# Shift and scale by column quarters, input projection by K quarters, in a one-core block of three feed-forward stages

## The chip, the core and the metric

The kernel runs on one core of a Trainium2 chip. The core has a matrix engine (PE), a vector engine (DVE), a scalar engine (ACT), a general engine (POOL) and a sync engine (SP), each with its own instruction stream, and 16 DMA engines that they share. Engines wait for one another through semaphores. The metric is the device time of one execution in microseconds (us), taken as a median of several runs.

## What is computed

The reference is a model block on a sequence of 256 rows of 2048 floats. Only its first part matters here:

```
mod = silu(c) @ w_ada + b_ada                      # w_ada: 2048 x 12288
shift1, scale1, gate1, shift2, scale2, gate2 = split(mod, 6)
h = rms_norm(x, norm1_w) * (1 + scale1) + shift1   # 256 x 2048
p = h @ w_in                                       # w_in: 2048 x 4112
u_f, q, k, v, o, gates = split(p)
y_f = real(fft2(u_f));  y_m = mlstm_bidirectional(q, k, v, gates) * sigmoid(o)
x = x + gate1 * (concat(y_f, y_m) @ w_out)
h2 = rms_norm(x, norm2_w) * (1 + scale2) + shift2
... three feed-forward blocks and a second mixer, all from h2 on
```

## The kernel before

Everything is float32. A product at nearly full precision is made of three matmuls on float32r operands: both operands are split into a high part (ACT, `w_hi`) and the rest (DVE, `w_lo`, "split"), and high by high, high by low and low by high are summed. Weights are read once from memory, in units of 1 MB (128 partitions by 2048 floats), into a ring of four slots, `stage`. SP issues these loads in one fixed order; each waits until the unit four before it in the ring is free. A unit that is split is free once DVE has made its low part (`split_made`); a unit that PE reads directly (of w_ada, since it meets only the one vector silu(c)) is free once PE has used it (`ada_used`). `w_hi` and `w_lo` hold two units each, so the split of unit n starts when PE has finished unit n-2.

The stages before the first feed-forward block are:

1. The front. SP loads the shift1 and scale1 columns of w_ada, 32 units of 128 rows by 2048 columns (`ada`, PE line 2643), 16 for each. The row of sums (four bands of 512, one bank of PSUM) is copied by DVE (`copy_sum`), turned into columns by PE (`turn_sum`, line 2655) and added to the bias (`take_sum`). Meanwhile x is normalized, its transposes are made (line 2492), and a table of small vectors comes in over POOL's queue and is transposed (line 2673).
2. The input projection. With shift and scale complete, DVE and ACT make the operand `xt` in eight groups (`norm_finish`). Then 16 units of w_in by column tiles (`in_tiles`, 128 columns by all of K, 48 matmuls of 256 columns each, lines 2394 to 2396), and 16 by rows (`in_rows`, 24 matmuls of 512 columns, lines 2443 to 2447). A result is accumulated in PSUM over all of K and copied once. Beside this, POOL issues the gate1 and scale-and-shift2 columns as 60 pieces of 512 KB into a ring of four (`late_ring`), and DVE multiplies and adds each into an accumulator (`late`, lines 1677 and 1678); four double pieces at the end go to PE. DVE's stream also carries the gates of the mLSTM.
3. The Fourier transform and the four mLSTM heads, with 16 units of scale2 columns that PE uses between them (`ada2`, `scale_units`).
4. The output projection `out1`, 16 units by rows; at its unit 9 DVE starts on the residual sum (`add_gated`), and the reload of x (POOL, line 531) has come by then.

The order on each engine is written by hand in the functions of `build`; nothing is reordered by a compiler.

## Time and profile before

| | us |
|---|---|
| median of 3 runs | 3562.35 |
| lowest and highest | 3561.05, 3566.18 |
| the profiled execution | 3561.49 |
| its span in the trace | 3559.6 |
| first matmul of the input projection | 108.5 |
| Fourier stage begins | 319.3 |
| out1 begins, ends | 387.1, 481.7 |

The span is counted from the first record of the trace; 1.9 us of the execution lie around it. PE is busy for 96% of the span, so a change can only shorten what lies in stretches in which PE is idle or does cheap work, above all the front. The trace lists for each instruction its start, its length and what ended the idle time before it. The granted clock of PE is either full (1.00) or half (0.50) in each moment; a window's value is the mean.

### The profile page before, as it was taken

The page shows a single profiled execution, that of the slowest core. Times are in us where ns is not written, and L with a number is a line of the kernel's source. Part 1 is how long each engine was busy: PE and PEld are TensorE (multiplying, and loading weights), DVE is VectorE, ACT ScalarE, POOL GpSimd, SP SyncE. Part 2 cuts the span into 40 slices and gives each one's busy share as a digit, 9 for nine tenths or more (in the row PEclk, how much of TensorE's full clock was granted, in tenths as well). Part 3 has the DMA queues.
Part 4 walks back from the last instruction along what each step waited for, and adds up shares of the span by engine and source line. Part 5 has one row for each costly group of instructions (what it writes and reads, how often), then busy time and mean ns, then how long its engine had stood idle before and what let it go on. Part 6 is the DMA issues. An engine that isn't in the chain of part 4 may idle for free.

```text
span 3559.6 us, 45278 instructions
## 1 busy us (share of the span) xinstructions
PE 3403.8 (96%) x18458; PEld 2863.0 (80%) x18458; DVE 2017.6 (57%) x2010; ACT 1528.3 (43%) x1554; POOL 346.1 (10%) x411
## 2 busy tenths in 40 slices
PE   5899889999999999999999899999999999999998
PEld 1786678888888888888888799898888788888886
DVE  0674657775566554444444579895455644444445
ACT  1333346653455443333333455663443443333333
POOL 1110000000000000000000137671000000000000
PEclk7899999999999999999999999999899999999999
DMA  9998657777666556976555655667226555665564
GB/s 398 296 340 311 219 172 224 223 223 226 189 187 192 189 196 177 207 199 197 193 189 189 166 150 157 168 174 249 86 96 191 175 189 189 189 190 190 190 190 139
DMA packets 543073, 713.09 MB, mean 200 GB/s; under 512 B 13127, under 2 KB 382079, under 8 KB 535360
## 3 DMA queue, kind: packets, MB, share of 16 engines
q1 hardware_dynamic: 517504, 627.09, 56.7%
q0 software_dynamic: 20624, 79.44, 7.9%
q10 hardware_dynamic: 4784, 4.27, 0.4%
q8 instruction: 120, 1.97, 0.2%
q14 instruction: 41, 0.34, 0.0%
HBM read 698.94 MB, written 11.80 MB: 200 GB/s over the span
## 4 chain that ended last, share of the span: by engine, by line
PE 79%; DVE 9%; ACT 4%; DMA 4%; issue 3%; POOL 1%; ACTq 0%; SPq 0%; DVEq 0%; POOLq 0%
PE ps L2585 9%; PE ps L2587 9%; PE ps L2586 9%; PE ps L2443 9%; PE ps L2444 8%; PE ps L2447 8%; PE ps L2375 7%; PE ps L2376 3%; DVE w_lo L1372 3%; ACT w_hi L812 3%; DMA stage<-in_w_ada 3%; PE ps L2394 2%; PE ps L2396 2%; PE ps L2395 2%; PE ps L2407 1%
## 5 line engine op out<-in xcount | busy, mean ns | idle before, releaser
L1372 DVE TENSOR_TENSOR w_lo<-stage,w_hi 128x2048 fp32r<-128x2048 f32 x528 | 1221.4, 2313 | 1176.0 <-ACT w_hi L812 1175.2
L812 ACT ACTIVATE w_hi<-stage 128x2048 fp32r<-128x2048 f32 x528 | 1010.7, 1914 | 1567.3 <-PE ps L2587 575.9
L2585 PE MATMUL ps<-w_hi,xt 128*128 128x512 f32 x1408 | 552.3, 392 | 3.4 <-DVE xt L1423 1.8
L2586 PE MATMUL ps<-w_lo,xt 128*128 128x512 f32 x1408 | 549.6, 390 | 0.0
L2587 PE MATMUL ps<-w_hi,xt 128*128 128x512 f32 x1408 | 549.6, 390 | 0.0
L2375 PE MATMUL ps<-xt,w_hi 128*128 128x512 f32 x1320 | 472.3, 400 | 6.2 <-DVE w_lo L1372 6.2
L2443 PE MATMUL ps<-w_hi,hid_hi 128*128 128x512 f32 x1152 | 449.6, 390 | 5.9 <-DVE w_lo L1372 5.9
L2444 PE MATMUL ps<-w_lo,hid_hi 128*128 128x512 f32 x1152 | 448.3, 389 | 0.0
L2376 PE MATMUL ps<-xt,w_lo 128*128 128x256 f32 x1320 | 371.3, 281 | 0.0
L2394 PE MATMUL ps<-xt,w_hi 128*128 128x256 f32 x1184 | 342.9, 290 | 18.6 <-DVE w_lo L1372 16.0
L2447 PE MATMUL ps<-w_hi,hid_lo 128*128 128x512 f32 x1152 | 354.6, 389 | 0.0
L2395 PE MATMUL ps<-xt,w_hi 128*128 128x256 f32 x1184 | 337.6, 285 | 0.0
L2396 PE MATMUL ps<-xt,w_lo 128*128 128x256 f32 x1184 | 337.4, 285 | 0.0
L2585 PEld LDWEIGHTS ps<-w_hi,xt 128*128 128x128 f32 x1408 | 265.4, 188 | 59.1 <-issue 2.3
L2587 PEld LDWEIGHTS ps<-w_hi,xt 128*128 128x128 f32 x1408 | 265.4, 188 | 55.6
L2586 PEld LDWEIGHTS ps<-w_lo,xt 128*128 128x128 f32 x1408 | 265.5, 189 | 54.7
L2375 PEld LDWEIGHTS ps<-xt,w_hi 128*128 128x128 f32 x1320 | 248.7, 188 | 66.9 <-DVE w_lo L1372 9.7
L2443 PEld LDWEIGHTS ps<-w_hi,hid_hi 128*128 128x128 f32 x1152 | 216.2, 188 | 52.6 <-DVE w_lo L1372 4.3
L2394 PEld LDWEIGHTS ps<-xt,w_hi 128*128 128x128 f32 x1184 | 229.5, 194 | 29.9 <-issue 23.6
L2376 PEld LDWEIGHTS ps<-xt,w_lo 128*128 128x128 f32 x1320 | 250.1, 189 | 3.6
L2447 PEld LDWEIGHTS ps<-w_hi,hid_lo 128*128 128x128 f32 x1152 | 216.2, 188 | 45.1
L2444 PEld LDWEIGHTS ps<-w_lo,hid_hi 128*128 128x128 f32 x1152 | 216.3, 188 | 44.4
(422 smaller groups left out, 4060.4 us busy)
## 6 DMA issues: line engine op xcount, KB each, us to landing
stage<-in_w_in SPq DMA_DIRECT2D x92, 1024.0 KB, 5.7
stage<-in_w_up SPq DMA_DIRECT2D x88, 1024.0 KB, 5.7
stage<-in_ffn_w_gate SPq DMA_DIRECT2D x88, 1024.0 KB, 5.1
stage<-in_ffn_w_up SPq DMA_DIRECT2D x88, 1024.0 KB, 5.1
stage<-in_ffn_w_down SPq DMA_DIRECT2D x88, 1024.0 KB, 5.4
stage<-in_w_ada SPq DMA_DIRECT2D x48, 1024.0 KB, 8.7
stage<-in_w_down SPq DMA_DIRECT2D x44, 1024.0 KB, 5.5
late<-in_w_ada POOLq DMA_DIRECT2D x64, 512.0 KB, 6.7
```

The lines of the kernel that those rows point to most:

```text
L812: act.activation(w_hi[:, u % 2 * UNIT:(u % 2 + 1) * UNIT], slot(u % SLOTS), ACT.Copy).then_inc(hi_made, 1)
L1372: dve.tensor_tensor(w_lo[:, part], slot(u % SLOTS), w_hi[:, part].bitcast(F32), ALU.subtract).then_inc(split_made, 1)
L2375: pe.matmul(dst, wh, both(k), start=k == 0, stop=False)
L2376: last = pe.matmul(dst[:, T:2 * T], wl, chunk(xt_hi, k), start=False, stop=False)
L2394: pe.matmul(dst, wh, chunk(xh, k0 + k), start=start and k == 0, stop=False)
L2395: pe.matmul(dst, wh, chunk(xl, k0 + k), start=False, stop=False)
L2443: pe.matmul(rows_cols(half, m, n, 512, swapped), a, wh, start=st, stop=False)
L2444: pe.matmul(rows_cols(half, m, n, 512, swapped), a, wl, start=False, stop=False)
L2447: last = pe.matmul(rows_cols(half, m, n, 512, swapped), b, wh, start=False, stop=en)
L2585: pe.matmul(dst, chunk(xt_hi, k, m), wh, start=k == 0, stop=False)
L2586: pe.matmul(dst, chunk(xt_hi, k, m), wl, start=False, stop=False)
L2587: last = pe.matmul(dst, chunk(xt_lo, k, m), wh, start=False, stop=k == KC - 1)
```

## The change

It changes only the stages up to and with out1.

- **Order of loads.** The 32 units of w_ada for shift1 and scale1 are cut otherwise: 512 columns by 512 rows, so that eight units (four of each) hold one quarter of shift and scale. w_in is cut the same way: unit n is K quarter n // 8, column block n % 8. The loads of quarter q+1 of w_ada and of K quarter q of w_in take turns (`IN_PLACE`, `ADA_PLACE`). All 32 units of w_in have 2 KB rows, where half had 512 B and half 4 KB.
- **The projection.** `in_unit` makes one K quarter of a block of 512 columns in a pair of banks. The first eight blocks are copied by ACT to where the result lies (`first_part`), the 24 others are added into it by DVE (`add_part`).
- **Quarters of shift and scale.** `turn_quarter` on PE sums the four bands with a matmul by `four_rows`, `quarter_scale`, `quarter_hi` and `quarter_lo` make four of the sixteen chunks of `xt`.
- **The rest of w_ada.** The shift2 columns, formerly pieces over POOL, are now units on SP's queue like scale2: `ada2` has 32 units instead of 16, eight in turns with the last K quarter, 24 between Fourier stage and heads. The gate1 pieces (32) remain, in a ring of two instead of four; DVE handles 8 in the last K quarter, 8 in the Fourier stage, 4 in the heads, 12 in out1. `fold_rows`, the turn and the bias of gate1 move from the projection into out1, between units 6 and 8, and PE waits for `mod_made` 7 before the second half. x is reloaded after that, and `add_gated` stands at unit 13 instead of 9.

On PE, the place is the end of the first loads of w_ada. Before, from the end of the 12th unit to the first matmuls of the projection (line 2643 is w_ada, 2492 the transposes of x, 2655 the turn of the sums):

```order
L2643 MATMUL ps<-stage,csilu 32x512 x8
L2492 MATMUL ps<-ident,f_nat 128x128 x16
L2643 MATMUL ps<-stage,csilu 32x512 x8
L2492 MATMUL ps<-ident,f_nat 128x128 x12
L2643 MATMUL ps<-stage,csilu 32x512 x64
L2655 MATMUL ps<-ident,mod_row_98 128x4 x4
L2655 MATMUL ps<-ident,mod_row_99 128x4 x4
L2492 MATMUL ps<-ident,f_nat 128x128 x4
```

After, from the fifth unit of w_ada on (2800 is w_ada, 2843 the table, 2615 the transposes of x, 2787 the turn, 2828 the projection):

```order
L2800 MATMUL ps<-stage,csilu 32x512 x20
L2843 MATMUL ps<-ident,rowtab 128x128
...
L2800 MATMUL ps<-stage,csilu 32x512 x12
L2615 MATMUL ps<-ident,f_nat 128x128 x8
L2787 MATMUL ps<-four_rows,mod_row_98 128x1 x4
L2787 MATMUL ps<-four_rows,mod_row_99 128x1 x4
L2828 MATMUL ps<-xt,w_hi 128x256
```

The projection stood behind 128 matmuls of w_ada and now stands behind 32; the table's transposes stand behind five units instead of twelve.

On DVE, the place is out1, from the last part of the operand on. Before (1372 is the split of a unit, 1451 and 1454 the residual sum):

```order
L1383 TENSOR_TENSOR xt_52<-turn_65,xt_52 128x2x256
L1372 TENSOR_TENSOR w_lo_51<-stage_49,w_hi_50 128x2048 x6
L1451 TENSOR_TENSOR f_nat_56<-ps,row_57 128x1024 x2
L1454 TENSOR_TENSOR x_nat_53<-x_nat_53,f_nat_56 128x1024 x2
L1372 TENSOR_TENSOR w_lo_51<-stage_49,w_hi_50 128x2048 x7
```

After (1447 is the split, 1753 a gate1 piece, 1781 and 1787 the copy of its sum and its bias):

```order
L1753 SCALAR_TENSOR_TENSOR acc_g1_106<-late1_101,csilu_62,acc_g1_106 128x1024
L1447 TENSOR_TENSOR w_lo_51<-stage_49,w_hi_50 128x2048
L1753 SCALAR_TENSOR_TENSOR acc_g1_106<-late0_100,csilu_62,acc_g1_106 128x1024
L1753 SCALAR_TENSOR_TENSOR acc_g1_106<-late1_101,csilu_62,acc_g1_106 128x1024
L1753 SCALAR_TENSOR_TENSOR acc_g1_106<-late0_100,csilu_62,acc_g1_106 128x1024
L1753 SCALAR_TENSOR_TENSOR acc_g1_106<-late1_101,csilu_62,acc_g1_106 128x1024
L1447 TENSOR_TENSOR w_lo_51<-stage_49,w_hi_50 128x2048 x2
L1781 COPY mod_row0_98<-ps 128x512
L1447 TENSOR_TENSOR w_lo_51<-stage_49,w_hi_50 128x2048
L1787 TENSOR_TENSOR mod_60<-ps,cols_59 128x16
L1447 TENSOR_TENSOR w_lo_51<-stage_49,w_hi_50 128x2048 x4
```

These rows are the splits of units 6, 7 and 8, 9 and the following; ahead of them a pair of pieces stands before each of the splits of units 4, 5 and 6. The splits stood alone before.

The diff, its core:

```
+IN_PLACE = (0, 2, 4, 6, 9, 12, 14, 15)
+ADA_PLACE = (1, 3, 5, 7, 8, 10, 11, 13)
+def in_place(n):
+    q, i = divmod(n, 8)
+    return 8 + 16 * q + (IN_PLACE[i] if q < 3 else 2 * i)
+def ada_place(a):
+    q, i = divmod(a, 8)
+    return i if q == 0 else 8 + 16 * (q - 1) + ADA_PLACE[i]
+def ada2_place(v):
+    return 57 + 2 * v if v < 8 else 64 + v
...
@@ SP
+        def fetch(at, src, whole, count, used):
+            if freed[at % SLOTS]:
+                sp.wait_ge(*freed[at % SLOTS])
+            ...
+            freed[at % SLOTS] = (used, count)
...
+        for v in range(8, 2 * KC):
+            fetch_ada2(v)
         load("out1", 8, 2, rows(I["w_out"], 0, 8))
@@ POOL
-        for n in (1, 2, 0, *range(3, 64)):
-            if n >= 4:
-                pool.wait_ge(S["late_acc"], n - 3)
...
+        pool.wait_ge(S["norm_xhat"], 2)
+        pool.wait_ge(split_used, 24)
+        for n in range(2):
+            late_piece(n)
...
+        for n in range(2, 32):
+            pool.wait_ge(S["late_acc"], n - 1)
+            late_piece(n)
+        pool.wait_ge(S["mod_made"], 7)
...
@@ ACT
+        def first_part(n):
+            act.wait_ge(split_used, n + 3)
+            for h in range(2):
+                last = act.activation(part_of(n, h), part_bank(n, h), ACT.Copy)
+            last.then_inc(S["tile_copied"], 1)
...
+            if 2 <= n < 10:
+                first_part(n - 2)
+            split_in(n)
+            if i == 0:
+                quarter_hi(q)
+            elif i == 7 and q < 3:
+                copy_sums(q + 1)
@@ DVE
+        for n in range(32):
+            q, i = divmod(n, 8)
+            if n >= 10:
+                add_part(n - 2)
+            if i == 0:
+                quarter_scale(q)
+            split_in(n)
+            if i == 0:
+                quarter_lo(q)
+            if q == 3:
+                late(i, 1)
...
+            late(8 + 2 * g, 2)
...
             last.then_inc(S["pt_made"], 1)
+            late(16 + h, 1)
...
         split("out1", 16, 0, 1)
+        late(20, 2)
...
+        late(22, 2)
         for u in range(4, 16):
             split("out1", 16, 0, u)
-            if u == 9:
+            if u < 6:
+                late(16 + 2 * u, 2)
+            elif u == 6:
+                late(28, 4)
+            elif u == 8:
+                copy_sum(7, 0, ADA + 2 * KC + 1)
+            elif u == 9:
+                take_sum(2, bank(7, 0, 16), 7)
+            if u == 13:
                 dve.wait_ge(S["x_in"], 32)
@@ PE
+        for q in range(3):
+            for step in range(16):
+                if step in IN_PLACE:
+                    i = IN_PLACE.index(step)
+                    in_unit(8 * q + i)
+                    if i == 2:
+                        norm(0, range(2 * q + 2, 2 * q + 4))
+                    elif i == 6:
+                        turn_quarter(q + 1)
+                else:
+                    ada(8 * (q + 1) + ADA_PLACE.index(step))
...
-            scale_units((0, 3, 6, 8)[g], (3, 3, 2, 2)[g])
+            for v in ((8, 9, 10), (11, 12, 13), (14, 15), (16, 17, 18))[g]:
+                ada2(v)
...
-                scale_units(10 + 2 * h, 2)
+                for v in ((19, 20, 21, 22, 23), (24, 25, 26, 27), (28, 29, 30, 31))[h]:
+                    ada2(v)
...
-        rows_half("out1", 8, 0, 0, at_out1, units=range(2, 8), ready=S["mix_lo"])
+        rows_half("out1", 8, 0, 0, at_out1, units=range(2, 7), ready=S["mix_lo"])
+        pe.wait_ge(S["late_acc"], 32)
+        fold_rows(7, late_acc[0][:, :])
+        rows_half("out1", 8, 0, 0, at_out1, units=range(7, 8), ready=S["mix_lo"])
+        turn_sum(7, 0, 0, 7)
+        pe.wait_ge(S["mod_made"], 7)
```

## Rows read from the trace of the kernel before

**Rows 1.** The profile's first page: the span.

```profile
span 3559.6 us, 45278 instructions
```

**Rows 2.** Windows by stage: bounds, length, busy us and count of each engine, PEclk, DMA share, GB/s.

```profile
0.00:44.00 44.00, 19.40 (x89) 2.58 (x89) 1.62 (x3) 8.96 (x9) 14.07 (x32) 0.75 0.98 374
44.00:108.50 64.50, 41.73 (x222) 12.10 (x223) 7.74 (x18) 3.17 (x3) 1.05 (x2) 0.69 1.05 393
108.50:319.30 210.80, 201.21 (x1274) 175.61 (x1274) 153.99 (x125) 76.83 (x64) 33.23 (x61) 0.98 0.94 314
319.30:387.10 67.80, 56.02 (x316) 32.86 (x312) 32.69 (x102) 23.01 (x51) 1.76 (x3) 0.92 0.83 310
387.10:481.70 94.60, 91.37 (x400) 74.52 (x400) 53.30 (x41) 34.53 (x29) 0.54 (x1) 0.98 0.58 179
```

**Rows 3.** Timeline of PE in the front: start, length, line, operation, idle before.

```profile
30.17 1.88 PE L2643 MATMUL ps<-stage,csilu 128*32 128x512 f32 x8 [0.54 <-DMA stage<-in_w_ada]
...
47.27 1.51 PE L2673 MATMUL ps<-ident,rowtab 128*128 128x128 f32 x6
...
99.53 3.57 PE L2655 MATMUL ps<-ident,mod_row 128*128 128x4 f32 x16 [0.81 <-DVE mod_row L1706]
...
108.52 0.55 PE L2394 MATMUL ps<-xt,w_hi 128*128 128x256 f32 x1 [3.88 <-DVE w_lo L1372]
```

**Rows 4.** Timeline of POOL and DVE in the front.

```profile
26.46 0.41 POOL L488 COPY rowtab<-hval 32x64 f32<-32x64 f32 x2 [16.58 <-DMA hval<-in_ssm_log_dt]
...
103.22 0.26 DVE L1712 TENSOR_TENSOR mod<-ps,cols 128x16 f32<-128x16 f32 x2 [3.74 <-PE ps L2655]
...
106.13 2.29 DVE L1372 TENSOR_TENSOR w_lo<-stage,w_hi 128x2048 fp32r<-128x2048 f32 x1
108.34 0.99 DVE L1528 TENSOR_SCALAR turn<-ps,scale_cols,mod 128x256 f32<-128x256 f32 x2
```

**Rows 5.** Timeline: two neighbouring high halves by tiles, two low halves in out1.

```profile
147.58 1.92 ACT L812 ACTIVATE w_hi<-stage 128x2048 fp32r<-128x2048 f32 x1 [3.58 <-PE ps L2396]
...
153.34 1.91 ACT L812 ACTIVATE w_hi<-stage 128x2048 fp32r<-128x2048 f32 x1 [3.58 <-PE ps L2396]
...
428.48 2.29 DVE L1372 TENSOR_TENSOR w_lo<-stage,w_hi 128x2048 fp32r<-128x2048 f32 x1 [3.15 <-ACT w_hi L812]
433.92 2.29 DVE L1372 TENSOR_TENSOR w_lo<-stage,w_hi 128x2048 fp32r<-128x2048 f32 x1 [3.15 <-ACT w_hi L812]
```

**Rows 6.** Groups by line, 108.4 to 319.3 us and Fourier to out1: busy, mean ns.

```profile
L1678 DVE SCALAR_TENSOR_TENSOR acc_g<-late,csilu,acc_g 128x1024 f32<-128x1024 f32 x30 | 37.6, 1280 | 2.8 <-DMA late<-in_w_ada 2.6
...
L2655 PE MATMUL ps<-ident,mod_row 128*128 128x4 f32 x16 | 2.0, 249 | 0.3 <-ACT mod_row L1061 0.3
```

**Rows 7.** DMA issues at 1700:1800, 125:215, 500:620, 300:345; last, FFN pieces: KB, us to landing.

```profile
stage<-in_ffn_w_gate SPq DMA_DIRECT2D x9, 1024.0 KB, 5.1
...
late<-in_w_ada POOLq DMA_DIRECT2D x33, 512.0 KB, 6.7
...
late_f<-in_w_ada POOLq DMA_DIRECT2D x12, 512.0 KB, 5.0
...
stage<-in_w_ada SPq DMA_DIRECT2D x12, 1024.0 KB, 7.9
...
DMA to landing us min/median/max: 3.9/4.9/9.1
```

**Rows 8.** Timeline of PE: Fourier stage begins, last scale2 unit, out1 begins.

```profile
319.34 3.72 PE L2746 MATMUL ps<-dft,projt 128*128 128x256 f32 x16
...
370.53 1.04 PE L2643 MATMUL ps<-stage,csilu 128*32 128x512 f32 x8
...
387.13 0.76 PE L2443 MATMUL ps<-w_hi,xt 128*128 128x512 f32 x1 [3.23 <-issue]
```

**Rows 9.** Windows: loads of w_ada with the queue full; a wait and the clock.

```profile
340.00:345.00 5.00, 4.07 (x35) 2.20 (x34) 1.53 (x3) 2.00 (x6) 0.00 (x0) 1.00 1.01 424
...
350.00:355.00 5.00, 3.91 (x6) 1.67 (x6) 3.80 (x11) 1.06 (x1) 0.00 (x0) 0.50 0.15 62
```

**Rows 10.** Timeline of DVE: the last low half of the operand in out1.

```profile
411.03 0.69 DVE L1383 TENSOR_TENSOR xt<-turn,xt 128x512 fp32r<-128x512 f32 x1 [0.70 <-ACT xt L1075]
```

More of the change, by code:

```diff
@@ L70, in stream_plan @@
 def stream_plan():
-    order = [("in_tiles", 16, 16), ("in_rows", 16, 16), ("ada2", KC, 0), ("out1", 16, 16)]
+    order = [("in", 32, 32), ("ada2", 2 * KC, 0), ("out1", 16, 16)]
     def ffn(n):
@@ new lines, in quarter_hi @@
+        def quarter_hi(q):
+            act.wait_ge(S["mod_made"], q + 1)
+            for g in (2 * q, 2 * q + 1):
+                act.wait_ge(S["norm_turned"], g + 1)
+                if g >= 2:
+                    act.wait_ge(S["norm_done"], g - 1)
+                c = 2 * g + 1
+                link.then(act.activation(turn[:, g % 2 * 512 + T:(g % 2 + 1) * 512], bank(5, g % 2 * T, T),
+                                         ACT.Identity, scale=scale_cols[:, c:c + 1], bias=mod[:, c:c + 1]))
+                act.wait_ge(S["norm_scaled"], g + 1)
+                act.activation(duo(xt_hi, g), turned_duo(g), ACT.Copy).then_inc(S["norm_hi"], 1)
@@ L1734, in _, with split_in @@
-        for b in range(2):
-            take_sum(b, bank(7, 16 * b, 16), 2)
-        scale_of(0)
-        norm_finish(0, scale_cols[:, 0:KC], mod[:, 0:16], lambda g: split("in_tiles", 4, 0, 0) if g == 2 else None)
-        piece = 0
-        for t in range(1, 16):
-            split("in_tiles", 4, t // 4, t % 4)
-            count = 0 if t < 2 else 3 if 6 <= t < 10 else 2
-            late(piece, count)
-            piece += count
-        dve.memset(v_one[:, :].rearrange("p (k n) -> p k n", n=257)[:, :, 256:257], 1.0)
+        def split_in(n):
+            dve.wait_ge(hi_made, n + 1)
+            part = slice(n % 2 * UNIT, (n % 2 + 1) * UNIT)
+            dve.tensor_tensor(w_lo[:, part], slot(in_place(n) % SLOTS), w_hi[:, part].bitcast(F32),
+                              ALU.subtract).then_inc(split_made, 1)
@@ L1798, in _ @@
-        dve.wait_ge(S["ec_made"], 1)
-        dve.tensor_copy(ecols[:, :], bank(2, 0, 32)).then_inc(S["ec_copied"], 1)
-        copy_sum(3, 0, ADA + 2)
+        for n in (30, 31):
+            add_part(n)
+        dve.wait_ge(S["f_act"], 2)
+        link.then(dve.scalar_tensor_tensor(out=two(lfrow[:, :]), in0=fgates, scalar=0.0,
+                                           in1=two(crow[:, :]), op0=ALU.min, op1=ALU.subtract))
+        for d in range(2):
+            last = dve.tensor_tensor_scan(way(rows1, 2 + d, d), ones1[:, :], way(lfrow, d, d), 0.0,
+                                          ALU.mult, ALU.add)
@@ L1801, in _ @@
+        link.then(last)
+        link.then(dve.tensor_tensor(two(rows1[:, 0:512]), igates, two(rows1[:, 512:1024]), ALU.subtract))
+        for d in range(2):
+            last = dve.tensor_tensor_scan(way(rows1, 4 + d, d), ones1[:, :], way(rows1, d, d), NEG,
+                                          ALU.mult, ALU.max)
+        link.then(last)
+        dve.tensor_tensor(rows1[:, 512:1024], rows1[:, 512:1024], rows1[:, 1024:1536],
+                          ALU.add).then_inc(S["f_dve"], 1)
         for g in range(4):
```

420 lines of the change are left out of this document (219 added, 201 removed).

## The prediction

> **What bounds the kernel now.** I read the windows by stage first [rows 2]. The front lasts 108.5 us; its DMA share is 0.98 and 1.05 while PE is busy in only 19.40 of 44.00 and 41.73 of 64.50 us, so loads bound it: nothing of the projection can start before 32 MB of w_ada are in. From 108.5 us to 319.3 PE is busy 201.21 of 210.80 us: the projection is bound by PE. The next stage, up to out1, is mixed (PE 56.02 of 67.80, DMA share 0.83). In out1 PE is busy 91.37 of 94.60 us, at a DMA share of 0.58. All later stages read what they read before, so the sum goes up to the end of out1, at 481.7 of a span of 3559.6 [rows 1].
>
> Then I read the timeline of the front, to see the chain that lets the projection start [rows 3, 4], the rhythm of the units [rows 5], the price of one piece or turn [rows 6], the time from issue to landing [rows 7], and two places in the tail [rows 8, 10].
>
> **Term 1, the start.** The eighth unit of w_ada is used at 30.17, with PE at half clock (1.88 us a unit) [rows 3]. The changed PE stream has the table's transposes after its fifth unit, and these wait for POOL's copy at 26.46 [rows 4]: 26.9, plus 1.5 for the transposes, plus three units of 1.9, is 34.1. Copies of two sums on ACT, bounded by 0.7 each (a DVE pass over as many columns, [rows 10]): 35.5. The transposes of x run beside them. The turn has eight matmuls, 3.57 at this clock [rows 3]: 39.1. Bias, scale and two affine steps, 0.26 + 0.2 + 0.2 + 0.99: 40.8. The split, 2.29, and the first low part, 0.7: 43.8 [rows 4, 10]. The first projection matmul comes at 43.8 instead of 108.52, so 64.7 us earlier. Were the first 2 KB-row loads as slow as one per 3 us, it would be 47.
>
> **Term 2, the projection.** Sixteen blocks with 256-column matmuls at 5.76 us (153.34 minus 147.58) and sixteen with 512 at 5.44 [rows 5] are 92.2 + 87.0 = 179.2, as before. The other 31.6 of the 210.8 us are 9.6 idle, six weighing units of 1.06, one turn of 1.0 (2.0 for two, [rows 6]), and 14.6 that stay: the gates' matmuls and stretches at half clock. New are 32 units of w_ada between the blocks, 33.9 at 1.06; three turns of eight matmuls, 6.0; 24 transposes of x, 3.0 (half of the 0.25 each that 1.51 for six gives at low clock). Copying and adding into place is on ACT and DVE: per unit DVE has 2.29 for the split and two additions of about 0.7, 3.7 of some 6.5 us, and the additions run while ACT makes the next high half, so I take nothing for them; with that cover gone they would cost 1.4 per unit.
>
> The ring adds a wait. The load of block 4 of a quarter takes the slot of a w_ada unit that PE uses just before block 3. From there a load of 5.1 [rows 7], the high half of 1.92 and the low half of 2.29 [rows 4, 5] make 9.4 us with the hops, while PE has only block 3 and two units, 7.9. That is 1.5 idle. Block 5 has the same pattern with 7.6 us of cover and a load that lands behind another one: about 1.9; block 6, after those waits, 0.6. Four us per quarter, three quarters, 12. Bounds: 6 with landings of 4.5, 27 with 6.7, which is what a smaller piece took beside other loads [rows 7]. I take 5.1, since these loads have the same shape, 2 KB rows, and 1 MB.
>
> Term 2 is 179.2 + 14.6 + 33.9 + 6.0 + 3.0 + 12 = 248.7, minus 0.6 for transposes that leave it: the projection ends at 291.9 instead of 319.3. Of the 64.7 us, 27.4 are left.
>
> **Term 3, Fourier stage and heads.** PE has 24 weighing units here instead of 16, and DVE 12 gate1 pieces on a queue of its own. With the queue full, DMA moves 424 GB/s at a share of 1.01 [rows 9], so 1 MB takes 2.49 us. Unit 8 is used about 4.2 us after the stage begins (two Fourier groups ahead of it); only then is unit 12 issued, and from there 20 MB for PE and 6 MB of pieces have to pass: 26 times 2.49 is 64.7. Add 3 us for the last landing and 1.1 for its use: 73.0. Before, out1 began 15.6 us after the end of the last such unit (387.13 minus 371.57, [rows 8]), and that chain is unchanged: 88.6 instead of 67.8, a loss of 20.8. Bounds: with room for everything only the eight more units count, 8.5; with DVE standing at `late` in front of `take_sum` and of the first exponents, which PE awaits through `mod_made` 5, another 5 on top.
>
> **Term 4, out1.** DVE reaches the end of the operand at 411.72 [rows 10]; with pieces 20 and 21 ahead of it I put 413.7 on the old scale. Then pieces 22 to 31. The ring holds two, so piece n is issued when n-2 is weighed, and one step costs a landing plus 1.28 [rows 6]. Landings were 6.7 in the projection and 5.0 in the feed-forward stage [rows 7]; out1 is nearer to the latter in load, so 5.2, a step of 6.5. Piece 22 is done at 415.0, 30 at 441.0, 31 at 442.3. The split of unit 7 stands behind them: 444.6; PE has then waited since unit 6. Unit 7 ends at 450.0. The second half waits for `mod_made` 7, which DVE sets only after the split of unit 9, and this waits for unit 7: 1.92 + 2.29 + 0.4 more, 454.6. Before, unit 8 began at 481.7 minus eight times 5.44, 438.2. A loss of 16.4, which I round to 17 with the wait that unit 3's split adds. Behind the waiting DVE are queued the splits that PE needs next; behind the waiting PE, all of the second half. The reload of x and the row of gate1 start then, with 3 MB or 7.5 us of transfer at 2.49 a MB [rows 9] and their latencies, and some 22 us before unit 12 is over: hidden; if not, `add_gated` delays the split of unit 14.
>
> **A rule of the Trainium skill against term 4.** These pieces took 5.0 and 6.7 us from issue to landing [rows 7]. The Trainium skill, "DMA: Bandwidth & Descriptors", section "Anatomy of one DMA — SWDGE (gpsimd) path", fits 2.0 us plus the bytes at 436 GB/s, which for 512 KB is an estimate of 3.2. With it the step would be 4.5, less than a unit, and DVE would keep up with PE; term 4 would be about 6.8. The trace does not agree for these queues, even its shortest landing is 3.9.
>
> **The sum.** 0 - 27.4 + 20.8 + 17 = +10.4. On the profiled execution's 3561.49 this gives 3571.9; the median of the runs lies 0.86 above the profiled one, so 3572.8, rounded to 3573. Later stages start from the same state and keep their lengths.
>
> **Rivals.**
> First, the pieces keep up. The shortest landing of a gate piece was 3.9 [rows 7]; with it a step is 5.2, under the 5.44 of a unit, DVE never holds PE, and term 4 is the fold and turn, 2.1, and the wait for `mod_made` 7, 4.6: 7. The sum is 0.4: 3563. Speaking for it is the DMA share of 0.58 in out1 [rows 2]; against it, that a median landing in a comparable load is 5.0. Chance 0.20.
>
> Second, landings are as long as where both queues are busy, 6.7 for a piece and 7.9 for a unit [rows 7]. Four steps cost 6 more, the ring of the projection 5 more: 3584. For it is that the projection has the pieces of the last quarter and loads at an even demand of 16 MB per some 60 us. PE waits of 3 to 5 us may also bring the clock down to half, as after the wait at 350 [rows 9], 2.5 us each. Chance 0.22.
>
> Third, and faster than before: the tail is bound by its chains, not by bytes. Then the 24 units and the pieces find room beside the four Fourier groups and the heads, term 3 is 8.5 and term 4 is 7: -27.4 + 15.5 = -11.9, 3551. It decides at 26 MB in some 52 us, 2.0 us each; the row at a share of 1.01 says 2.49, so the chance is 0.08.
>
> My forecast, 3566 to 3581, has 0.50. That the change does not start the projection early is excluded by PE's order.
>
> **How the numbers follow.** A measurement of this kernel can tell 0.2%, 7.1 us, from no change. Slower by more: 0.40 of the forecast (above 3569.5) and all of the second rival, 0.62. Within: 0.10 of the forecast, 0.17 of the first rival, 0.27. Faster: 0.03 of the first and 0.08 of the third, 0.11. The range takes in the first rival and most of the second, 3554 to 3591; the third, and a second rival at its bounds for all terms, are left out.
>
> **What would show it.** In the changed profile: first projection matmul at 44 (wrong above 50); projection over by 292, with PE idle 1 to 2 us for `w_lo` at blocks 4 and 5 of each of three quarters; out1 beginning at 380; DMA share near 1 in the stage before; PE waiting in out1 between units 6 and 7 for more than 5 us and between 7 and 8 for 3 to 4; out1 ending at 492. The prediction is wrong if the weighing units between the blocks cost more than 1.06, if additions on DVE end after the next high half, or if the pieces land in under 4.2 us.

## The result and the profile after

The changed kernel takes 3600.34 us (median of 4 runs, 3599.45 to 3602.30); the kernel before took 3562.96 beside it. The ratio is 1.0105, with a 95% interval of 1.0087 to 1.0122: slower by 37.4 us, where the prediction was slower by 10.4, in a range that ended at 3591. The sign was right, the size was not, and the time lies above every case that was worked out.

The windows of the changed kernel, cut at the same events as [rows 2]: first projection matmul, first Fourier matmul, first scores of the heads, first matmul of out1, last of out1. The columns are bounds, length, busy us and count of each engine, PEclk, DMA share, GB/s.

```profile
0.00:45.30 45.30, 21.07 (x95) 6.70 (x95) 7.29 (x19) 15.36 (x17) 13.43 (x30) 0.97 0.99 347
45.30:302.10 256.80, 239.21 (x1539) 188.81 (x1539) 120.24 (x118) 80.59 (x73) 6.39 (x12) 0.97 0.79 280
302.10:346.80 44.70, 31.05 (x201) 19.19 (x201) 21.29 (x30) 13.02 (x28) 3.71 (x7) 0.81 0.93 372
346.80:404.90 58.10, 44.52 (x184) 21.89 (x185) 30.57 (x92) 12.79 (x22) 2.64 (x5) 0.76 0.80 301
404.90:518.40 113.50, 99.72 (x416) 79.10 (x416) 68.40 (x55) 34.62 (x29) 7.74 (x13) 0.91 0.72 215
```

The same cut of the kernel before, whose last-but-one stage is split here at its first scores:

```profile
319.30:345.60 26.30, 25.37 (x189) 16.01 (x185) 5.37 (x11) 7.61 (x25) 1.06 (x2) 1.00 0.91 362
345.60:387.10 41.50, 30.65 (x129) 16.85 (x128) 27.32 (x91) 15.40 (x26) 0.70 (x1) 0.87 0.78 277
```

Stage by stage the change gives 63.2 us in front, and costs 45.9 in the projection (256.7 instead of 210.8), 18.4 in the Fourier groups, 16.7 in the heads and 18.9 in out1; 1.4 lie behind out1. The sum is +38.1, the difference of the spans (3597.7 and 3559.6). Against the forecast the misses are: start +1.5, projection +8.6, groups and heads together +14.3 (102.9 for 88.6), out1 +1.9 (113.5 for 111.6), the rest +1.4.

The start is as forecast, at 45.34 for 43.8 (timeline of PE; answers to [rows 3]):

```profile
45.34 0.55 PE L2828 MATMUL ps<-xt,w_hi 128*128 128x256 f32 x1 [4.51 <-DVE xt L1458]
```

Where PE waited behind the projection (waits of PE, 302 to 520 us: who waited, for whom, us in total, times, longest):

```profile
PE ps L2766 <- DMA stage<-in_w_ada: 12.5, 6, 3.8
PE ps L2924 <- DVE mod L1787: 8.5, 1, 8.5
PE ps L2766 <- DVE acc_g L1753: 5.3, 1, 5.3
PE ps L2564 <- DVE w_lo L1447: 4.8, 4, 2.9
PE ps L2564 <- DVE mod L1787: 3.7, 1, 3.7
```

The second row is the largest single wait. This is what DVE did before it (timeline of DVE: pieces 12 and 13, the last low part of the Fourier groups, pieces 14 and 15, the sum):

```profile
333.26 1.28 DVE L1753 SCALAR_TENSOR_TENSOR acc_g<-late,csilu,acc_g 128x1024 f32<-128x1024 f32 x1 [1.86 <-DMA late<-in_w_ada]
337.02 1.28 DVE L1753 SCALAR_TENSOR_TENSOR acc_g<-late,csilu,acc_g 128x1024 f32<-128x1024 f32 x1 [2.48 <-DMA late<-in_w_ada]
...
340.26 0.69 DVE L1458 TENSOR_TENSOR xt<-turn,xt 128x512 fp32r<-128x512 f32 x1 [0.69 <-ACT xt L1126]
343.08 1.28 DVE L1753 SCALAR_TENSOR_TENSOR acc_g<-late,csilu,acc_g 128x1024 f32<-128x1024 f32 x1 [2.12 <-DMA late<-in_w_ada]
345.35 1.28 DVE L1753 SCALAR_TENSOR_TENSOR acc_g<-late,csilu,acc_g 128x1024 f32<-128x1024 f32 x1 [0.99 <-DMA late<-in_w_ada]
346.55 0.17 DVE L1787 TENSOR_TENSOR mod<-ps,cols 128x16 f32<-128x16 f32 x1
```

and the other side of it (timeline of PE):

```profile
334.47 3.77 PE L2908 MATMUL ps<-dft,four 128*128 128x129 f32 x16
346.77 2.07 PE L2924 MATMUL ps<-rows,sel 4*128 4x512 f32 x2 [8.53 <-DVE mod L1787]
```

DVE stands at landings in front of a 0.17 us addition that signals PE. The turn that this addition reads was done at 334.6. In the runs without pieces in this stage (e1, e2 below) PE still waits 2.86 us at this place, so 5.7 of the 8.53 belong to the pieces.

While PE waits and then makes the first scores it uses no unit of w_ada, and the loads fall off (windows of the changed kernel; then waits of SP's queue, 300 to 405 us):

```profile
340.00:350.00 10.00, 3.23 (x5) 1.55 (x6) 4.37 (x7) 4.92 (x5) 1.06 (x2) 0.50 0.69 240
350.00:360.00 10.00, 9.38 (x40) 2.87 (x39) 4.81 (x11) 2.11 (x2) 0.53 (x1) 0.66 0.37 113
```

```profile
SPq L428 <- PE ps L2766: 71.3, 21, 23.6
```

The longest wait of the queue for PE to free a slot was 23.6 us. Ahead of that the landings had grown, against 7.9 of [rows 7] for a unit (DMA issues at 300:345; KB, us to landing):

```profile
stage<-in_w_ada SPq DMA_DIRECT2D x12, 1024.0 KB, 10.2
late<-in_w_ada POOLq DMA_DIRECT2D x7, 512.0 KB, 8.2
```

Two queues each ask for as much as their buffers allow, and each transfer takes longer from issue to landing; without the pieces (e2, 299 to 340 us) a unit lands in 8.2. The Trainium skill, "DMA: Bandwidth & Descriptors", section "Queues, rings and completion order", says that every DMA engine takes turns between the queues that have work for it; by that a piece on one queue delays a unit on the other. The 10.2 us with pieces and the 8.2 without are in line with it.

### The profile page after: what moved, and what is told of

Its sections match the earlier page's. It is cut to its first block, busy times and chain, and to the rows that moved or that the text cites. A ratio compares the mean times of both kernels' runs of the same rounds, so it can differ in the third digit from the quotient of the medians.

```text
span 3597.7 us, 45458 instructions
## 1 busy us (share of the span) xinstructions
PE 3429.0 (95%) x18594; PEld 2881.3 (80%) x18594; DVE 2014.4 (56%) x2034; ACT 1538.4 (43%) x1567; POOL 327.0 (9%) x379
## 4 chain that ended last, share of the span: by engine, by line
PE 78%; DVE 9%; ACT 5%; DMA 4%; issue 3%; POOL 1%; ACTq 0%; SPq 0%; DVEq 0%; POOLq 0%
PE ps L2708 9%; PE ps L2710 9%; PE ps L2709 9%; PE ps L2564 7%; PE ps L2565 7%; PE ps L2568 7%; PE ps L2496 7%; PE ps L2497 3%; DVE w_lo L1447 3%; ACT w_hi L877 3%; PE ps L2515 2%; PE ps L2516 1%; PE ps L2517 1%; DMA stage<-in_w_ada 1%; DMA stage<-in_w_in 1%
## 5 line engine op out<-in xcount | busy, mean ns | idle before, releaser
L1447 DVE TENSOR_TENSOR w_lo<-stage,w_hi 128x2048 fp32r<-128x2048 f32 x496 | 1144.8, 2308 | 1138.8 <-ACT w_hi L877 1138.1
L877 ACT ACTIVATE w_hi<-stage 128x2048 fp32r<-128x2048 f32 x496 | 949.6, 1914 | 1399.3 <-PE ps L2710 575.9
L2497 PE MATMUL ps<-xt,w_lo 128*128 128x256 f32 x1320 | 371.2, 281 | 0.0
L2496 PEld LDWEIGHTS ps<-xt,w_hi 128*128 128x128 f32 x1320 | 248.7, 188 | 66.9 <-DVE w_lo L1447 10.0
L2515 PE MATMUL ps<-xt,w_hi 128*128 128x256 f32 x928 | 266.6, 287 | 8.9 <-DVE w_lo L1447 8.9
L2516 PE MATMUL ps<-xt,w_hi 128*128 128x256 f32 x928 | 262.9, 283 | 0.0
L2517 PE MATMUL ps<-xt,w_lo 128*128 128x256 f32 x928 | 262.8, 283 | 0.0
L2565 PEld LDWEIGHTS ps<-w_lo,hid_hi 128*128 128x128 f32 x1152 | 216.3, 188 | 44.6
L2515 PEld LDWEIGHTS ps<-xt,w_hi 128*128 128x128 f32 x928 | 178.3, 192 | 17.4 <-issue 17.4
```

Source lines behind the costliest of these rows:

```text
L877: act.activation(w_hi[:, u % 2 * UNIT:(u % 2 + 1) * UNIT], slot(u % SLOTS), ACT.Copy).then_inc(hi_made, 1)
L1447: dve.tensor_tensor(w_lo[:, part], slot(u % SLOTS), w_hi[:, part].bitcast(F32), ALU.subtract).then_inc(split_made, 1)
L2496: pe.matmul(dst, wh, both(k), start=k == 0, stop=False)
L2497: last = pe.matmul(dst[:, T:2 * T], wl, chunk(xt_hi, k), start=False, stop=False)
L2515: pe.matmul(dst, wh, chunk(xh, k0 + k), start=start and k == 0, stop=False)
L2516: pe.matmul(dst, wh, chunk(xl, k0 + k), start=False, stop=False)
```

## Experiments

Each run is compared with the kernel before on the same chip. That kernel took 3561.1 us (median) beside e1 to e4, 3563.0 beside e5 to e8, 3564.7 beside e9 to e11 with both e10, and 3562.7 beside e12 to e15, so times of different groups are best compared by their ratios. The table has the profiled execution of each, cut at the events named above: first projection matmul; length of projection, Fourier groups up to the first scores, heads, out1; span; then the ratio of its runs to those of before.

| kernel | start | proj. | groups | heads | out1 | span | ratio (95%) |
|---|---|---|---|---|---|---|---|
| before | 108.5 | 210.8 | 26.3 | 41.5 | 94.6 | 3559.6 | 1 |
| after | 45.3 | 256.7 | 44.7 | 58.2 | 113.5 | 3597.7 | 1.0105 (1.0087 to 1.0122) |
| e1_early | 44.7 | 268.6 | 32.9 | 57.6 | 103.0 | 3587.6 | 1.0069 (1.0053 to 1.0086) |
| e2_no_pieces | 45.2 | 253.9 | 32.8 | 55.8 | 103.0 | 3570.2 | 1.0035 (1.0020 to 1.0050) |
| e3_order | 46.7 | 258.0 | 39.6 | 58.7 | 116.1 | 3598.6 | 1.0117 (1.0101 to 1.0134) |
| e4_ring | 45.7 | 255.1 | 45.8 | 58.6 | 113.8 | 3598.0 | 1.0106 (1.0089 to 1.0123) |
| e5_act | 46.7 | 257.4 | 45.4 | 60.3 | 113.6 | 3601.0 | 1.0109 (1.0093 to 1.0124) |
| e6_warm | 44.8 | 254.5 | 46.7 | 58.0 | 113.5 | 3600.2 | 1.0106 (1.0091 to 1.0122) |
| e7_combo | 46.8 | 261.2 | 35.8 | 55.7 | 99.0 | 3579.5 | 1.0047 (1.0034 to 1.0061) |
| e8_combo_ring | 46.7 | 271.7 | 36.0 | 55.6 | 97.0 | 3585.7 | 1.0056 (1.0042 to 1.0070) |
| e9_ring6 | 44.9 | 240.7 | 44.8 | 56.8 | 116.3 | 3584.6 | 1.0068 (1.0053 to 1.0084) |
| e10_no_mm | 44.8 | 250.1 | 33.5 | 57.3 | 103.6 | 3572.5 | 1.0020 (1.0011 to 1.0030) |
| e10_gone | 46.6 | 250.6 | 23.5 | 58.5 | 103.1 | 3563.2 | 0.9997 (0.9988 to 1.0007) |
| e11_full | 45.1 | 248.3 | 30.5 | 49.6 | 94.7 | 3546.0 | 0.9965 (0.9951 to 0.9979) |
| e12_spread | 46.4 | 251.1 | 40.6 | 44.4 | 96.0 | 3559.3 | 0.9976 (0.9967 to 0.9985) |
| e13_act2 | 46.7 | 251.3 | 30.5 | 50.1 | 94.7 | 3551.0 | 0.9970 (0.9959 to 0.9981) |
| e14_spread_np | 44.8 | 250.5 | 42.6 | 44.8 | 103.5 | 3564.1 | 1.0020 (1.0010 to 1.0030) |
| e15_spread_act | 44.6 | 250.6 | 37.5 | 44.3 | 95.9 | 3552.4 | 0.9965 (0.9953 to 0.9977) |

How exact one execution is can be read from it: after, e3, e5 and e6 have the same code up to the Fourier groups, and their projections take 254.5 to 258.0. With pieces beside it the projection varies more: e1 and e7 have the same code up to its end and take 268.6 and 261.2. So differences of a stage under 4 us say little, and under 8 in a projection with pieces. The profiled executions of e8 and e12 were the slowest of their runs (3.3 and 9.0 us above the median), that of e11 the fastest.

**What the pieces cost: e1 and e2.** e1 gates the first pieces at `split_used` 3 instead of 24 and puts `late` behind every unit from 2 on (the diff); e2 has the same lines taken out and only `late(0, 2)` in the last quarter.

```
-            if q == 3:
-                late(i, 1)
+            if n >= 2:
+                late(n - 2 + (n > 12) + (n > 20), 2 if n in (12, 20) else 1)
...
-            late(8 + 2 * g, 2)
...
-            late(16 + h, 1)
```

> The changed kernel, with the 24 gate1 pieces that it weighs in the Fourier stage, the heads and out1 moved into the projection: one piece behind each unit from unit 2 on, same ring of two. Theory A (what the changed kernel loses behind the projection is the price of those pieces: their bytes on a full queue, and DVE standing for their landings in front of what PE awaits): the stage from the first Fourier matmul to out1 falls from 102.9 us to 80 to 88, out1 loses its waits of 22.7 us on DVE and about 18 of its 115 us, the projection stays within 3 of 256.7; about 3562. Theory B (the eight more weighing units of w_ada on PE and the single ring of four cost that stage its time, whatever DVE loads): the stage stays above 98, only out1 gains; about 3578.

> The changed kernel with 30 of the 32 gate1 pieces left out (gate1 is wrong for it; nothing else is left out): 15 MB less to load. This is the bound of what the pieces can cost anywhere. Theory A: 3555 to 3562, at most 5 below the kernel with the pieces moved early, since the projection has room for them (DMA share 0.75 to 0.80). If the pieces cost as much beside the projection as in the tail, this one is 15 or more below the other. Theory B: the stage from the first Fourier matmul to out1 stays above 98 here too; about 3578.

Measured: 3588.08 and 3572.04, so the pieces cost 27.5 us in the changed kernel and 17.4 moved early (spans 3597.7, 3587.6, 3570.2); by the ratios of the runs it is some 25 and 12. Neither theory is right as it stood. Out1 gave back 10.5 in both, the groups 12 (the 8.53 us wait is 2.86 now). The 18 us that theory A expected of out1 were taken from 22.7 us of waits; those are DVE's own waits for pieces from 300 to 520 us. PE's waits for DVE in out1 were 13.7. And the projection, at a DMA share of 0.76 without pieces, did not take them for nothing: it is 14.7 longer with them in e1, and 7.3 longer in e7, which has the same projection. And the heads keep their 56 to 58 us with no piece at all. The stage that was forecast at 88.6 with 12 pieces takes 88.6 without any.

**The order on DVE: e3.** The fold is taken ahead of pieces 14 and 15.

```
-            late(8 + 2 * g, 2)
+            if g < 3:
+                late(8 + 2 * g, 2)
...
         exponents(0)
+        late(14, 2)
```

> The changed kernel, with only the order on DVE changed at one place: pieces 14 and 15 are weighed after the shift's fold is taken (which sets the mod_made 5 that PE waited 8.53 us for) and after the first exponents. Bytes and number of pieces are the same. If DVE's standing in front of that signal is what held PE, out1 begins 4 to 8 us earlier than at 404.9 and the time is about 3594. If the bytes of the stage hold it, the wait comes back at a weighing unit for its load, out1 begins within 2 us of 404.9: 3599 to 3600.

Measured: 3602.35, no gain. The wait at the scores fell from 8.53 to 3.78, the groups are 5.1 shorter and the heads 0.5 longer. By its start (403.04 instead of 404.92) out1 would fit the second reading, but this execution was 2.6 us behind when its Fourier stage began, in code that the edit leaves as it was; counted from there out1 begins 4.5 us sooner, which fits the first. What was gained is gone in out1, 116.1 for 113.5, with waits no longer than in the changed kernel. At a spread of 4 us one execution does not settle whether the stage gained, and why nothing of it reaches the time stays open.

**Slots, not places: e4 and e9.** e4 changes the two tuples of places; e9 gives the 24 loads of w_ada beside the projection two slots of their own, in `x_nat`, which is free there.

```
-IN_PLACE = (0, 2, 4, 6, 9, 12, 14, 15)
+IN_PLACE = (0, 2, 4, 6, 8, 10, 14, 15)
-ADA_PLACE = (1, 3, 5, 7, 8, 10, 11, 13)
+ADA_PLACE = (1, 3, 5, 7, 9, 11, 12, 13)
```

```
     def slot(s):
+        if s >= SLOTS:
+            return x_nat[:, (s - SLOTS) * UNIT:(s - SLOTS + 1) * UNIT]
         return stage[:, s * UNIT:(s + 1) * UNIT]
```

> The changed kernel, with only the places in the ring of four changed: within a quarter the eight blocks take places 0, 2, 4, 6, 8, 10, 14, 15 and the eight loads of w_ada 1, 3, 5, 7, 9, 11, 12, 13, so that the loads of blocks 4 and 5 take slots which a block's low part freed more than one block before, not slots that PE used just before block 3. If the ring is the cause of the idle time before blocks 4, 5 and 6 (14.8 us in 9 waits), 8 to 12 of it go, and the projection ends at 290 to 294 instead of 302.1. If the loads are simply slower than PE (landing time, bandwidth), the waits only move to other units and less than 3 us go. The stage behind is at a DMA share of 0.93, so part of a gain may be given back there: 3588 to 3592 by the first, 3598 by the second.

> The changed kernel with a deeper ring for its first part: the 24 loads of w_ada beside the projection land in two slots of their own (16 KB per partition that x_nat leaves free there), the four slots of stage serve the blocks of w_in alone, and each load is issued when PE or DVE frees a slot of its kind. From the last quarter on all is as in the changed kernel. Another order of four slots had moved the waits and taken none. If the projection is short of slots (a load of 7.2 to 7.4 us in flight against what four slots leave), the waits of 14.8 us go below 3, the projection ends near 289 instead of 302, and the time is 3586 to 3589. If it is short of bandwidth (DMA share 0.75 to 0.80 there) or bound by DVE's and ACT's splits, they stay above 8: 3595 or more.

Measured: 3599.69 and 3588.41. In e4 the waits ahead of blocks 4 and 5 are gone and a longer one stands ahead of block 6 of each of the first three quarters (4.00, 3.83, 3.76), with a block behind it that runs in part at half clock (timeline of PE, e4, first quarter: a matmul takes 0.63 us where it takes 0.39 at full clock):

```profile
88.54 2.78 PE L2800 MATMUL ps<-stage,csilu 128*32 128x512 f32 x24
95.32 0.79 PE L2834 MATMUL ps<-w_hi,xt 128*128 128x512 f32 x1 [4.00 <-DVE w_lo L1811]
95.91 0.63 PE L2835 MATMUL ps<-w_lo,xt 128*128 128x512 f32 x1
```

e4 fits its second reading, e9 its first: the nine waits of 14.8 for a block's low part are two of 2.2. In e9 the projection is 16.0 us shorter, at a higher DMA share and clock (window of e9's projection):

```profile
44.90:285.60 240.70, 232.90 (x1538) 184.49 (x1538) 120.65 (x118) 79.93 (x73) 6.39 (x12) 0.99 0.84 300
```

The blocks' loads land no sooner, in 7.7 us (7.4 in the changed kernel), those of w_ada in 5.4 (7.2); there are more of them under way. So the projection was short of slots, and the price of that is 9.7 us of idle time and 6.3 of lower clock (PE busy 239.2 against 232.9, granted clock 0.97 against 0.99). e9 does three things in one: two slots more, a ring of its own for w_ada, and the first pieces held back until the last of these loads is used. Which part of the 16 each of them has was not tested. Some 3 us of it were lost again behind it.

**ACT's order and the clock: e5 and e6.** e5 moves `split("out1", 16, 0, 0)` behind the exponential of head 3. e6 adds 16 matmuls that nobody reads ahead of the wait for `mod_made` 5.

```
-            if h >= 2:
-                split("out1", 16, 0, h - 2)
+            if h == HEADS1 - 1:
+                split("out1", 16, 0, 0)
+                split("out1", 16, 0, 1)
```

```
+        for _ in range(16):
+            pe.matmul(bank(0), chunk(xt_hi, 12, 0), both(12), start=True, stop=True)
         pe.wait_ge(S["mod_made"], 5)
```

> The changed kernel, with only ACT's order changed in the heads: the first split of out1 comes behind the exponential of head 3 and the copy of the sum of w_ada, no longer ahead of them. In the changed kernel ACT stood 9.20 us there for the first load of w_out, which the ring hands out only behind the last loads of w_ada, and PE then waited 1.77 for the copy and 1.12 for pt. If that stand is on the path, out1 begins 3 to 7 us earlier than at 404.9: about 3595. If only PE's last waits count (1.77 + 1.12), or the split then comes late for out1's own first unit, 0 to 2: 3599.

> The changed kernel, with 16 matmuls of 512 columns added whose result nobody reads, in the place where PE waited 8.53 us for mod_made 5; all else is the same. It asks what the idle time costs beyond its own length. If PE's wait is what brings the granted clock to half behind it (the first scores took 2.07 us at half clock, 1.12 at full), the stretch from 347 to 360 runs at full clock and out1 begins 2 to 4 us earlier: about 3597. If the clock does not follow this wait, or the stretch is bound by DVE and the loads, nothing: 3600; if the added work delays the scores, up to 3604.

Measured: 3602.81 and 3601.81; neither gained. In e5 the wait for the copy (1.77) is gone, and PE waits 3.65 for `pt` instead of 1.12. That is not the split, whose low half DVE makes only behind `pt`: DVE writes `pt` of the last head after it has taken the result of the head before from PE (timeline of DVE, e5), a chain that the edit does not touch. The wait for the copy had stood beside it.

```profile
396.88 0.35 DVE L1964 TENSOR_SCALAR dcols<-ps 128x1 f32<-128x1 f32 x4 [8.38 <-PE ps L2948]
...
399.82 1.41 DVE L1948 SCALAR_TENSOR_TENSOR pt<-ps,ex 128x256 f32<-128x256 f32 x4
```

In e6 the added work was done and the scores ran at half clock all the same (timeline of PE, e6), so what that wait costs beyond its own length stays open:

```profile
336.69 4.89 PE L2919 MATMUL ps<-xt 128*128 128x512 f32 x16
345.98 2.07 PE L2926 MATMUL ps<-rows,sel 4*128 4x512 f32 x2 [4.41 <-DVE mod L1787]
```

**Repairs of order on top of e1: e7 and e8.** The edit of e5, and in out1 the fold after unit 4 and the turn after unit 6; e8 adds the places of e4.

```
-        rows_half("out1", 8, 0, 0, at_out1, units=range(2, 7), ready=S["mix_lo"])
+        rows_half("out1", 8, 0, 0, at_out1, units=range(2, 5), ready=S["mix_lo"])
         pe.wait_ge(S["late_acc"], 32)
         fold_rows(7, late_acc[0][:, :])
+        rows_half("out1", 8, 0, 0, at_out1, units=range(5, 7), ready=S["mix_lo"])
+        turn_sum(7, 0, 0, 7)
         rows_half("out1", 8, 0, 0, at_out1, units=range(7, 8), ready=S["mix_lo"])
-        turn_sum(7, 0, 0, 7)
```

> The kernel with the gate1 pieces moved into the projection (3588.08), with two changes of order more: the split order on ACT of the run before last, and in out1 the fold of gate1 after unit 4 and its turn after unit 6 in place of 6 and 7, so that mod_made 7 is set before the second half asks for it. The second takes away the wait of 3.68 us and its half clock, about 4 to 5. The first takes away most of the wait of 5.74 for the copy of the sum, about 4. Theory: 3588 - 4.5 - 4 = about 3579.5. Rival (the waits come back at the load of the next unit): 3586.

> The kernel just described, with the ring places 0, 2, 4, 6, 8, 10, 14, 15 for blocks as well. In that order alone three waits of 3.9 us before block 6 stood for nine shorter ones, and the time stayed. If what the projection loses is set by the time a load takes from issue to landing (8.5 us beside the pieces) against a ring of four handed out in order, this is within 2 of the kernel without it; if the order of places matters once landings are longer, 4 to 6 lower.

Measured: 3580.71 and 3584.12. Out1 falls from 103.0 to 99.0, so the wait for `mod_made` 7 was worth its length. That e7 met its 3579.5 is otherwise luck: the split's new place gave no 4 us (groups and heads together 91.5 for 90.5, and 3.65 at `pt` again), while the projection, which neither edit touches, came out 7.4 shorter than in e1. e8's projection is 10.5 longer than e7's, and its time higher by 3.4 with intervals that overlap: the other places gain nothing with pieces beside them either.

**Why the stage is long without pieces: e10, e14.** e10 and e14 start from e2. In the first e10, units 8 to 15 of w_ada, the first eight of the stage, are one matmul of one column each, in the second their loads go too. e14 moves four units from the heads to the groups.

```
+            if 8 <= v < 16:
+                pe.matmul(bank(2, 500, 1), ident[:, :], ones_col[:, :], start=True, stop=True).then_inc(S["ada_used"], 1)
+                return
```

```
-            for v in ((8, 9, 10), (11, 12, 13), (14, 15), (16, 17, 18))[g]:
+            for v in ((8, 9, 10, 11), (12, 13, 14, 15), (16, 17, 18, 19), (20, 21, 22))[g]:
...
-                for v in ((19, 20, 21, 22, 23), (24, 25, 26, 27), (28, 29, 30, 31))[h]:
+                for v in ((23, 24, 25), (26, 27, 28), (29, 30, 31))[h]:
```

> The kernel without the 30 gate1 pieces (3572.04, its stage from the first Fourier matmul to out1 88.6 us against 67.8 of before), and with it eight of the stage's 24 weighing units reduced on PE to one small matmul of 0.25 us; their loads stay. (shift2 is wrong for it.) If PE's own work is what the change adds to the stage, it gets 6 us shorter, more with the clock: 80 to 83. If the loads are, PE waits the saved time again: 87 to 89.

> As the run before, but the eight loads of 1 MB are left out too, so that the stage has the 16 units that the kernel before has there. If the loads bind, the whole 20.8 us go: 68 to 72 for the stage, about 3553. If the stage is longer for the way that the change arranges it (signals, turns, DVE's work, clock) it stays above 78.

> The kernel without the 30 gate1 pieces (3572.04; stage 88.6 us), with four weighing units moved from the heads to the Fourier groups as in the first of these runs. With four slots the loads of the Fourier groups are at a DMA share of 1.02 already, so four more there cost their 2.49 us each, 10 us, while the heads have four fewer. If the place of the units is the cause, the heads (55.8 us from the first scores to out1) fall to 46 to 48, and the stage to 84 to 87. If the loads bind wherever the units stand, the stage stays at 88 to 90.

Measured stages from first Fourier matmul to out1: 90.8, 82.0 and 87.4, against 88.6 of e2 and 67.8 before. PE's work for eight units is worth nothing (e10_no_mm); their loads are worth 7 to 9 us; 14.2 remain with the 16 units that the kernel before has, so the loads are not the whole of the 20.8 (the second reading of that run). In those 14.2 PE is busy 9.3 us longer for the same units (65.3 for 56.0, at a granted clock of 0.76 in the heads for 0.87) and idle 5 us longer. The length is in the heads, 58.5 us for 41.5, with the groups 2.8 shorter: PE takes 13 units there instead of six, and while it is at the first scores the four slots are full with units it will only take later, so that DMA all but stops (window of e10_gone; the row of the kernel before that answers it stands at 0.31, 350 to 360 us):

```profile
320.00:330.00 10.00, 7.41 (x12) 3.16 (x12) 4.64 (x13) 5.57 (x5) 0.00 (x0) 0.54 0.23 97
```

With nine units in the heads, e14 has them at 44.8, which is close to the 41.5 of before and three units of 1.06. The groups pay 9.8 for it, because there one unit comes per 2.49 us (timeline of PE, e14), a megabyte at the full rate of [rows 9]:

```profile
310.06 1.06 PE L2756 MATMUL ps<-stage,csilu 128*32 128x512 f32 x8 [1.41 <-DMA stage<-in_w_ada]
312.55 1.06 PE L2756 MATMUL ps<-stage,csilu 128*32 128x512 f32 x8 [1.42 <-DMA stage<-in_w_ada]
```

So with 24 loads the place decides which part is long and hardly the sum, 87.4 for 88.6. That the place also makes the 14.2 that are left with 16 loads is argued from the share of 0.23; no run has 16 units in the places of before.

**A version that beats both: e11, and three variants.** Six slots for w_ada up to the last unit (the last 24 take the four slots of stage and the two in `x_nat` in turn); all 32 gate1 pieces in the projection, with buffers in `four` and `f_nat` and the sum in `row`; gate1 folded at the projection's end. The core of the planner, run once when the program is built:

```
+def in_x(kind, n):
+    if kind == "ada2" and TAIL_X:
+        return n < 8 or (n - 8) % 6 >= 4
+    return kind == "ada" and n >= 8
...
+        for it in items:
+            x = in_x(*it)
+            if rings[x]:
+                fetch(*rings[x].pop(0))
```

> Everything together, as a version meant to beat both: two more slots for the loads of w_ada throughout (the last 24 units take six slots in turn), all 32 gate1 pieces weighed in the projection with their own two buffers elsewhere and gate1 folded at its end, so that none is left in the stage behind it or in out1. Against the best so far (3580.71): projection 263.3 us to about 246, the stage from 91.5 to about 87, out1 from 99.0 to 96.5: about 3558. If the pieces lengthen the projection for bandwidth and not for slots, its 263 stay near 258 and it ends at 3570 to 3575.

> The fastest kernel so far (3549.74), with four weighing units moved: 4, 4, 4 and 3 of them stand with the four Fourier groups and 3 with each head, for 3, 3, 2, 3 and 5, 4, 4. Same loads, same work. If the units in the heads are what makes the heads long (49.6 us from the first scores to out1, against 41.5 before), these get 4 to 6 shorter and the Fourier groups (27.7) 4.2 longer, plus what PE then waits there for loads: a net of 0 to -3, 3547 to 3550. If the loads of the Fourier groups bind once more of them are asked for there, +3: 3553.

> The fastest kernel so far (3549.74), with ACT's first split of out1 behind the exponential of head 3 and the copy of the sum. PE waited 2.00 us for that copy and 1.33 for pt. If the split stands on the path, out1 begins 2 to 3 us earlier: 3547. If not, as in the changed kernel, where the same edit gave nothing: 3549 to 3550.

> The two edits together on the fastest kernel. If both count: 3544 to 3547, the best of all. If neither: 3549 to 3550.

Measured: 3549.74, 3552.12, 3552.04 and 3551.33. e11 is faster than the kernel before by 0.35% (interval 0.21 to 0.49), 12 to 15 us, and 8 us below its expectation; its runs spread from 3547.8 to 3558.9. The surplus is in the stage of groups and heads, 80.1 us where 87 was expected. Its windows:

```profile
45.10:293.40 248.30, 238.31 (x1546) 186.61 (x1546) 149.80 (x141) 80.07 (x73) 17.50 (x33) 0.97 0.94 345
293.40:323.90 30.50, 27.66 (x212) 18.03 (x208) 12.24 (x24) 9.04 (x25) 0.53 (x1) 1.00 0.93 362
323.90:373.50 49.60, 38.53 (x184) 19.17 (x185) 25.78 (x88) 16.65 (x26) 1.87 (x2) 0.83 0.81 299
373.50:468.30 94.80, 91.56 (x400) 74.70 (x400) 53.38 (x41) 34.62 (x29) 0.57 (x1) 0.98 0.67 198
```

The projection carries the pieces at a DMA share of 0.94, which the kernel before had in that stage too [rows 2], and out1 is back at 94.7, for 94.6 before. The variants are inside its spread, so none of their expected gains came. e12 has the edit of e14 (and one wait of PE moved ahead of the third group's units), e13 that of e5, e15 both. e12 repeats what e14 showed: heads 5.2 shorter, groups 10.1 longer (7.0 in e15 against e13). e13 takes the wait for the copy away and gets 3.65 at `pt`, as e5 did.

## Why the prediction was wrong

**Term 1, the start: right.** 45.3 for 43.8.

**Term 2, the projection: mechanism right, size off.** The blocks that wait are the ones named, 4, 5 and 6 of three quarters (2.37, 2.01 and 2.36 us at block 4, 1.17, 2.94 and 0.76 at block 5, and 1.22, none and 1.52 at block 6). The term mis-sized is "four us per quarter, 12". Its input was a landing of 5.1, taken because the loads have the same shape; they took 7.2 and 7.4, and the slots too few cost 16.0 (e9), 6.3 of it in half clock, which the step had left out. The other 4.6 of the miss are what e9 still has above 236.1, the forecast without its 12. It has waits of 7.5 in all that the sum did not name: 2.4 for the gates' rows, 2.9 for loads, 2.2 for splits.

**Term 3, groups and heads: the step that failed.** It is "from there 20 MB for PE and 6 MB of pieces have to pass: 26 times 2.49 is 64.7". This takes DMA to be full from the use of unit 8 to the last landing. It is full from 312 to 342 us; then it is not, with shares of 0.69 and 0.37 in the windows from 340 to 360, since four slots cannot take loads that are used later. The last unit was used 85.8 us after the stage began (387.82 less 302.06) where the step has 73.0, and out1 came 17.1 behind it for 15.6. That is the miss of 14.3.

As a sum the price of the pieces was right in the same step. With e2's bytes it gives 4.2, 20 times 2.49, 3, 1.1 and 15.6, which is 73.7; e2 took 88.6. So the step falls short by 14.9 without pieces and by 14.3 with them, and the 14.9 that it had for their 6 MB compare with 14.3 measured (after less e2). DVE's stand was in the prediction as a bound, "another 5 on top"; it was 5.7 (8.53 less the 2.86 that stay without pieces). It is not what empties the queue: in e2 the share is as low, 0.29 and 0.55 from 330 to 350 us.

Of the 35.1 us that the stage lost, PE's busy time has 19.6 (75.6 for 56.0), of which eight units of 1.06 are 8.5 and the rest goes with a lower clock (0.81 and 0.76, for 1.00 and 0.87), and its idle time 15.4. The step had a price for neither the clock nor the empty time of the queue. By runs they are 14.3 the pieces, 6.6 the eight more loads (e2 less e10_gone) and 14.2 that stay with the bytes of before. The last are put down to the 13 units in the heads, where the kernel before had six, and to the clock behind the waits; their parts stay open.

**Term 4, out1: right, in part by luck.** 113.5 for 111.6. Pieces landed in 5.0 for the 5.2 assumed; the waits forecast between units 6 and 7 and behind unit 7 are there (5.30, 3.68; timeline of PE):

```profile
458.00 1.94 PE L2766 MATMUL ps<-acc_g,ones_col 128*32 128x512 f32 x8 [5.30 <-DVE acc_g L1753]
```

But by the working unit 6 ended at 432.8 (438.2 less 5.44) and PE stood up to 444.6, less the 2.1 of fold and turn, so nearly 10 us; the wait was 5.3. PE's longer busy time made up for it, 99.7 for 91.4 at a granted clock of 0.91 for 0.98, and the term has nothing for the clock. The reload of x was hidden, as forecast: PE's wait behind the residual sum is the 0.61 us of before.

**The rivals.** The second, long landings, was the nearest at 3584: landings were as long as it said in the projection (7.2 to 7.4 for its 7.9) and longer in the stage between (8.2 and 10.2, for its 6.7 and 7.9), where it priced nothing; in out1, where it had 6 us for them, pieces landed in 5.0. The third, a tail bound by chains with room for the bytes, is not borne out: in e10_no_mm and e14 PE's work and its place change and the stage stays at 87 to 91 us, while eight loads less take 7 to 9 off. The first, pieces that keep up with PE, would have held for out1 had they landed in 3.9; they took 5.0. The range ended at 3591; no case in it had the loads fall off in the stage between.

## What to carry to other kernels

Count the loads that can be under way, not only bytes and the share of the queue: at a share of 0.79 a ring of four left PE waiting, and two slots more in memory that lay idle, with a ring of their own, took 16 us from the same stage. A price per byte on a full queue holds only while the slots let the queue be full. When a ring feeds one consumer, loads placed for late use stop it early. A helper that waits for a landing must not stand in front of a short instruction that another engine awaits, though mending that alone (e3) did not shorten the kernel here. Before a wait is taken away, look for the chain beside it: in e5 the next one took its place.
